# Norms of the second network taken tile by tile: squares on ACT from PSUM, transposes by tile in two banks, the next weight split between the tiles

## The reference

```python
def block(x, ...):                       # 256 x 1024
    sh1, sc1, ga1, sh2, sc2, ga2 = modulation(c)
    h = rmsnorm(x, g_mix_pre) * (1 + sc1) + sh1
    y = hybrid_mixer(h)                  # h @ w_in (1956 wide), 3 kinds of attention, @ w_out
    x = x + ga1 * rmsnorm(y, g_mix_post)
    h = rmsnorm(x, g_ffn_pre) * (1 + sc2) + sh2
    y = swiglu(h)                        # h @ w_gate_up (2 x 2816), silu(g) * u, @ w_down
    x = x + ga2 * rmsnorm(y, g_ffn_post)
```

## Time and profile before

| | us |
|---|---|
| median of 3 runs | 2006.28 (2004.70 to 2008.29) |
| profiled execution, its own time | 2009.39 |
| its span in the trace | 2007.6 |
| PE busy | 1788.9 (89%) |
| DVE busy | 1121.1 (56%) |
| ACT busy | 688.0 (34%) |
| POOL busy | 96.2 (5%) |
| mean granted clock of PE | 0.917 |

### The profile page before, as it was taken

One profiled execution on the slowest core, in us unless ns is written; L12 is line 12 of the kernel. 1 busy time (PEld: TensorE's weight loads), 2 busy tenths in 40 slices (PEclk: granted clock), 3 DMA queues, 4 the chain that ended last, 5 costly groups with the idle time before them and its releaser, 6 DMA issues.

```text
span 2007.6 us, 25506 instructions
## 1 busy us (share of the span) xinstructions
PE 1788.9 (89%) x10612; PEld 1454.1 (72%) x10612; DVE 1121.1 (56%) x1727; ACT 688.0 (34%) x811; POOL 96.2 (5%) x91
## 2 busy tenths in 40 slices
PE   5998888789999999988879996997899979879997
PEld 2775646677877777775558995775799756759996
DVE  3475454564445445555477675555766565566654
ACT  2323333132222122423334443454333333534331
POOL 1010001110000000010010000000100010010000
PEclk8999877899999999897889998898899989879999
DMA  8324455124333344334754545450555554325642
GB/s 325 124 86 168 169 197 202 42 75 149 133 126 126 129 159 144 105 136 147 257 192 171 203 175 206 151 190 10 161 187 164 180 199 152 126 63 182 196 159 93
DMA packets 172371, 309.20 MB, mean 154 GB/s; under 512 B 3264, under 2 KB 54720, under 8 KB 171616
## 3 DMA queue, kind: packets, MB, share of 16 engines
q1 hardware_dynamic: 168592, 293.98, 42.1%
q10 hardware_dynamic: 3376, 12.02, 1.8%
q0 software_dynamic: 288, 1.57, 0.2%
HBM read 305.46 MB, written 2.10 MB: 153 GB/s over the span
## 4 chain that ended last, share of the span: by engine, by line
PE 69%; DVE 16%; ACT 5%; issue 5%; DMA 3%; POOL 1%; DVEq 0%; ACTq 0%; SPq 0%; POOLq 0%
PE bank L535 53%; PE twin L535 14%; DVE ring_r L1159 4%; DVE arena L1159 3%; PE bank L544 3%; ACT arena L1884 2%; ACT arena_r L1884 2%; DMA ring<-in_w_in 2%; DMA ring<-in_w_mod 2%; POOL rs L2235 1%; DVE params L1159 1%; DVE arena_r L1159 1%; DVE X L1636 1%; DVE params L1622 0%; DVE arena L1249 0%
## 5 line engine op out<-in xcount | busy, mean ns | idle before, releaser
L535 PE MATMUL bank<-arena_r 128*128 128x512 f32 (+3 forms) x2144 | 710.2, 377 | 14.5 <-DVE arena_r L1754 6.7
L1159 DVE TENSOR_TENSOR ring_r<-ring,arena_r 128x4096 fp32r<-128x4096 f32 (+4 forms) x94 | 393.7, 4188 | 233.3 <-ACT arena_r L1884 232.7
L535 PEld LDWEIGHTS bank<-arena_r 128*128 128x128 f32 x2144 | 412.2, 192 | 95.8 <-issue 7.9
L1884 ACT ACTIVATE arena_r<-ring 128x4096 fp32r<-128x4096 f32 (+4 forms) x94 | 323.0, 3436 | 432.9 <-PE bank L535 160.5
L535 PE MATMUL twin<-actT_r,arena_r 128*128 128x256 f32 x1408 | 254.5, 284 | 1.2 <-DVE actT_r L1159 1.2
L535 PE MATMUL bank<-arena_r,actT_r 128*128 128x512 f32 (+4 forms) x640 | 227.1, 386 | 25.7 <-DVE ring_r L1159 14.2
L535 PE MATMUL bank<-ring_r,arena_r 128*128 128x512 f32 x624 | 246.0, 394 | 0.0
L1884 ACT ACTIVATE arena<-bank 128x512 f32<-128x512 f32 (+6 forms) x170 | 85.7, 504 | 426.2 <-PE bank L535 329.8
L535 PEld LDWEIGHTS twin<-actT_r,arena_r 128*128 128x128 f32 x1408 | 219.8, 192 | 2.0 <-DVE actT_r L1159 2.0
L535 PE MATMUL twin<-actT_r,ring_r 128*128 128x256 f32 x704 | 199.2, 283 | 0.0
L535 PE MATMUL bank<-ring_r,actT_r 128*128 128x512 f32 (+4 forms) x512 | 191.7, 374 | 0.0
(11 more groups left out here) (183 smaller groups left out, 1753.0 us busy)
## 6 DMA issues: line engine op xcount, KB each, us to landing
ring<-in_w_mod SPq DMA_DIRECT2D x24, 2048.0 KB, 8.0
ring<-in_w_ada SPq DMA_DIRECT2D x24, 2048.0 KB, 8.2
ring<-in_w_gate_up SPq DMA_DIRECT2D x44, 1024.0 KB, 7.7
ring<-in_w_down SPq DMA_DIRECT2D x20, 2048.0 KB, 7.8
ring<-in_w_up SPq DMA_DIRECT2D x16, 2048.0 KB, 7.8
ring<-in_w_in SPq DMA_DIRECT2D x12, 2048.0 KB, 8.7
ring<-in_w_out SPq DMA_DIRECT2D x8, 2048.0 KB, 11.7
ring<-in_w_down SPq DMA_DIRECT2D x8, 1792.0 KB, 7.5
```

The lines of the kernel that those rows point to most:

```text
L535: ins = nc.tensor.matmul(out_, lhsT, rhs, start=start, stop=stop)
L1159: return v.tensor_tensor(o, x, y, op)
L1884: return nc.scalar.activation(o, x, func, **kw)
```

## The change

Six things change, all for the second network:

1. `residual2`: DVE no longer copies the banks nor squares them. ACT squares the sums straight from PSUM (`squares2`), with the accumulated sum in `ss`, and DVE multiplies straight from the bank by `GA`, once `gsq_ready` says that ACT's square is there.
2. `residual2` now does in half 1, for tile 0 and then tile 1: half of the next weight's split (`split_part`), the scaling, the addition to `X`, and `norm_tile`. For tile 1 `turned2(0)` stands between the addition and the norm.
3. PE transposes a tile at a time (`normed2` on PE): feature tiles 0 to 3 of tile t in one v bank, 4 to 7 in one a bank, in a burst of 8 for t = 0 and one for t = 1.
4. `turned2(t)` on DVE and `normed2` on ACT empty these: four 128x128 scale-and-shift each, one rounding copy of 128x512 each, and two subtractions of 128x512, both on DVE. POOL has no part in it any more.
5. The next product waits for `act_ready`: for `in2` 0 its first tile of tokens needs only tile 0; for `up2` 0, which takes both tiles at once, the first feature tile needs the third and the fifth the fourth of the four signals.
6. In `loads()` the first `mod2` chunk of a layer stands behind `in2` 0 instead of ahead of it.

```diff
-        out += [("par2a", l, 0)] + take(1) + ins[:3] + [("par2b", l, 0)] + take(1) + ins[3:] + take(2)
+        out += [("par2a", l, 0)] + ins[:1] + take(1) + ins[1:3] + [("par2b", l, 0)] + take(1) + ins[3:] + take(2)
```

PE, the transposes (here and below B's call stands for the three):

```diff
+            def normed2(n):
+
+                for t in range(TS):
+                    pe.wait_ge(xn_ready, nth(xn_ready))
+                    for g, r in enumerate("va"):
+                        b, filled = take(r)
+                        for i in range(4):
+                            ft = 4 * g + i
+                            tr(b[:, i * P:(i + 1) * P], normal(n)[:, t, ft * P:(ft + 1) * P], filled if i == 3 else None)
...
-                normed([0, 1], 2 * (L + l) + 1)
+                mark["y", l, 1] = k["v"]
+                normed2(2 * (L + l) + 1)
```

DVE:

```diff
+            def turned2(t):
+
+                c = slice(t * P, (t + 1) * P)
+                b = filled()
+                for ft in range(4):
+                    step(v.tensor_scalar(act2_lo[:, ft, c], b[:, ft * P:(ft + 1) * P], modT[:, 1, ft, 0:1],
+                                         modT[:, 0, ft, 0:1], ALU.mult, ALU.add), v_emptied if ft == 3 else v_step)
+                step(v.tensor_copy(actT_r[:, 0:4, c], act2_lo[:, 0:4, c]))
+                rest(act2_lo[:, 0:4, c], act2_lo_r[:, 0:4, c], actT_r[:, 0:4, c], act_ready)
+                dve.wait_ge(high_ready, nth(high_ready))
+                rest(act2_lo[:, 4:8, c], act2_lo_r[:, 4:8, c], actT_r[:, 4:8, c], act_ready)
...
             def last_norm(t):
+                if t == 1:
+                    turned2(0)
                 dve.wait_ge(sq_ready, nth(sq_ready))
...
                 for half in range(2):
                     c = slice(half * MODC, (half + 1) * MODC)
                     for key in keys[half]:
-                        split(after(key))
+                        if key != keys[1][-1]:
+                            split(after(key))
...
                     for t in range(TS):
-                        b = filled()
-                        y = y2[:, t, c]
-                        step(v.tensor_copy(y, b[:, :]), v_emptied)
-                        squares(junk2, y, t)
...
+                        if half and late:
+                            split_part(late, t, False)
+                        scaled(t, half)
+                        if half:
+                            added(t)
+                            if n and t == 1:
+                                turned2(0)
+                            if n:
+                                norm_tile(t, n)
+                if n:
+                    turned2(1)
```

ACT, where `squares2` is called once for each half, behind the last high part of that half:

```diff
+            def squares2(l, stage, half):
+
+                n = mark["y", l, 2 * stage + half] - 2
+                for t in range(TS):
+                    act.wait_ge(v_filled, n + t + 1)
+                    step(f(junk2, VB[(n + t) % 2][:, :], ACT.Square, accum_out=ss[:, 2 * half + t:2 * half + t + 1]),
+                         gsq_ready)
+
+            def normed2(n):
+
+                for t in range(TS):
+                    squared([t], n)
+                    if t == 0:
+                        act.wait_ge(modT_ready, nth(modT_ready))
+                    c = slice(t * P, (t + 1) * P)
+                    b = filled()
+                    for i in range(4):
+                        step(f(act2_lo[:, 4 + i, c], b[:, i * P:(i + 1) * P], ACT.Identity, scale=modT[:, 1, 4 + i, 0:1],
+                               bias=modT[:, 0, 4 + i, 0:1]), a_emptied if i == 3 else a_step)
+                    step(f(actT_r[:, 4:8, c], act2_lo[:, 4:8, c], ACT.Copy), high_ready)
```

More of the change, by code:

```diff
@@ L570, in three, with linear @@
                 mm(out_, lhs[1], rhs[0], False, last, inc)
-            def linear(out_, lhs, rhs, inc, order=range(KT)):
+            def linear(out_, lhs, rhs, inc, order=range(KT), turned={}):
                 for i in order:
+                    if i in turned:
+                        pe.wait_ge(act_ready, nth(act_ready, turned[i]))
                     if k["turned"]:
@@ L1225, in split, with split_part @@
                             ALU.subtract), w_ready)
-            def split_part(key, part):
-                if part:
+            def split_part(key, part, parted=True):
+                if part or not parted:
                     dve.wait_ge(whi_ready, SPLITS.index(key) + 1)
@@ L1607, in squares, with residual2, scaled, added @@
                                             op1=ALU.add, accum_out=ss[:, at:at + 1]))
-            def residual2(keys, behind):
+            def residual2(keys, late, n):
                 dve.wait_ge(ga_in, nth(ga_in, 32))
+                def scaled(t, half):
+                    c = slice(half * MODC, (half + 1) * MODC)
+                    b = filled()
+                    mean = ms[:, t:t + 1]
+                    dve.wait_ge(gsq_ready, nth(gsq_ready))
+                    if half == 0:
+                        step(v.tensor_scalar(mean, ss[:, t:t + 1], 1.0 / D, EPS, ALU.mult, ALU.add))
+                    else:
+                        v.scalar_tensor_tensor(out=mean, in0=ss[:, 2 + t:3 + t], scalar=1.0 / D, in1=mean,
+                                               op0=ALU.mult, op1=ALU.add).then_inc(ms_ready, 1)
+                        handed.append(("power", t, 1))
+                    step(tt(y2[:, t, c], b[:, :], GA[:, 0, c], ALU.mult), v_emptied)
+                def added(t):
+                    dve.wait_ge(rstd_ready, nth(rstd_ready))
+                    step(v.scalar_tensor_tensor(out=X[:, t, :], in0=y2[:, t, :], scalar=rs[:, t:t + 1],
+                                                in1=X[:, t, :], op0=ALU.mult, op1=ALU.add), x_ready)
                 for half in range(2):
@@ L1619, in residual2 @@
                     for t in range(TS):
[L1620 to L1639 removed]
+                        if half and late:
[9 more added lines that the diff above has]
+                    turned2(1)
             def layer2(l):
[L1642 removed]
+                if l == 0:
+                    turned2(1)
                 split(after(("in2", l, 0)))
@@ L2205, in layer2 @@
                     split(after(("down2", l, c)))
+                    if c % 3 == 2:
+                        squares2(l, 1, c // 3)
             act.dma_start(cons[:, :], a["cons"]).then_inc(cons_in, 16)
```

43 lines of the change are left out of this document (16 added, 27 removed).

## The result

The changed kernel is slower: 2022.1 us (median of 7 runs, 2014.18 to 2026.03) against 2006.2 us for the kernel before (7 runs, 1999.5 to 2009.31). The ratio is 1.0075, 95% interval 1.0058 to 1.0093. The forecast was 2015.4 with a range up to 2021.5: the median lies 0.6 above that end, and the ratio, on the 2006.28 that the forecast was made from, gives 2021.3, just inside it.

A forecast was written before the change was run, and what follows sets the result against it. PE was taken as the bound (busy 89%, chain of waits 69% on PE, 16% on DVE). A -0.8, B and D +10.0, C +1.9, E -2.0 sum to +9.1, on the median 2006.28 giving 2015.4 us; range 2006.5 to 2021.5.

The forecast's parts named there:

- B: PE's idle time ahead of the norm's transposes between `out2` and `up2` in layer 0; predicted +5.0 us.
- F: The time at which the last product of `out2` ends, from which the prediction counts its chain of steps.
- A: PE's idle time ahead of the transposes before `in2` 0 in layer 0; predicted -6.3 + 5.5 = -0.8 us.
- D: The same place as B in layer 1, taken as its twin; predicted +5.0 us.
- C: The same place as A in layer 1; predicted -2.0 - 0.3 + 4.2 = +1.9 us.
- E: The kernel's end, where DVE's copy and square of tile 1 go; predicted 1.7 earlier and 0.3 for half 0: -2.0 us.
- Rival 3: PE stays at the low clock 7 us behind each burst pair; B and D lose 2.5 more each, C 2: 2022; chance 0.13.
- (i): At B and D, ScalarE's order holds tile 0's norm back until behind F; mending it gives about -6 us in all.
- (ii): At B and D, the half split of 2.3 us stands on the path; splitting whole gives -4.7 us in all.
- (iii): At B and D, `turned2(0)`'s 3.6 us stand in the way of tile 1's norm; reordering gains 7 us in all.
- (iv): At A and C, `in2` 2 is late because its load takes `in2` 0's slot; the old order removes 5.9 us waits: 2019 to 2023.

## Why the prediction was right, and where not

**The direction and the mechanism were right.** At B each step of the chain came where the prediction put it:

| step | predicted | measured |
|---|---|---|
| square of `X` tile 0 there | F + 2.3 | F + 2.0 |
| norm of tile 0 | F + 4.0 | F + 3.6 |
| half split | F + 6.2 | F + 6.0 |
| addition of tile 1 | F + 8.7 | F + 8.2 |
| `turned2(0)` | F + 12.2 | F + 11.9 |
| norm of tile 1 | F + 13.8 | F + 13.5 |
| four transposes of tile 1, seen by VectorE | F + 15.1 | F + 14.8 |
| first product | F + 17.9 | F + 17.8 |

That the last step fits within 0.1 is partly luck, since small errors cancel: ScalarE's two squares were 0.3 shorter than I had put them, the four 128x128 took 1.75, not 1.45, and the rounding copy 0.43, not 0.6.

**The terms**, in the first pair of profiles: A -0.6 (predicted -0.8), B +5.6 (+5.0), D +6.2 (+5.0), C +1.5 (+1.9), E -0.3 for half 0 and -1.9 for the last addition (-2.0 together). `in2` 2's product came at S + 19.9 in both layers, predicted S + 19.2, with S the issue of its load.

That A and C fit so well is luck. At A the first product with `in2` 0 came 7.3 sooner, not 6.3, and what followed cost 6.8, not 5.5. At C S came 2.8 sooner, not 2.0, and the rest cost 4.6, not 4.2. I had overlooked that the load of `in2` 2 waits not for the last product with `in2` 0 but for the first one with `in2` 1, 1.3 and 1.6 us later. And C is +1.5 only beside the first profile of before, where the clock fell from 1679 to 1683; beside the second, where it did not, it is +3.4.

With 1.6 for `down2` behind D (below) the terms add up to 12.2, and the pair differs by 8.6. The other 3.6 lie between the places, where no instruction differs: 1.1 ahead of B, 1.5 ahead of C, where before the clock fell from 1587 to 1591, and 1.0 ahead of D. At E the addition ends 3.1 us behind the last product (which ended at 2004.85) where it was 5.0 (1998.17), as this row shows beside the earlier trace rows:

```profile
2006.66 1.28 DVE L1661 SCALAR_TENSOR_TENSOR X<-params,rs,X 128x1024 f32<-128x1024 f32 x1
```

**The term that was mis-sized is the clock.** I had put 0.9 at each of B and D. The 1056 products took 128.7 us at B and 129.3 at D, and 126.9 where they ran at the high level throughout (at D with TensorE kept busy): 1.8 and 2.4. `down2`'s second half behind D took 1.6 more as well: in both profiles of the changed kernel the clock fell again there, in neither of before. This is that place in the first one:

```profile
1974.00:1976.00 2.00, 2.00 (x6) 1.51 (x6) 0.00 (x0) 1.92 (x1) 0.00 (x0) 0.52 0.75 254
```

But this fall is no sure part of the price. In both profiles of before the same fall of 3.4 us stands in `down2` of layer 0, 174 us behind F at B, and in neither of the changed kernel; and the changed kernel with the whole split, or with the loads of before, has it in neither layer. The runs show that such a fall comes at the same place in both profiles of a kernel, not what sets it off.

Rival 3 had the direction, that the clock costs more than 0.9, and the total, 2022, but not by its own working: it wanted 2.5 more at each of B and D, which were 0.9 and 1.5, and 2 more at C.

**What stays open.** The medians lie 15 to 16 us apart, the stretches behind A give 8.6 to 9.9. So the sum, 9.1, fits what lies behind A and not the whole difference. Some 3 us more lie ahead of A, where no instruction differs: the pass ended at 1235.8 to 1245.4 (mean 1242.0) in the eight profiles of kernels whose work by tile begins at A and at 1235.6 to 1240.1 (mean 1238.9) in the five others. The difference is TensorE's clock between 300 and 400 us and between 1000 and 1100 us, where TensorE is busy at the low level for 24 to 36 us, and for 8 to 16. Both ends occur in both groups. Whether the change shifts their odds, or eight against five profiles were luck, is not settled; nor are the last 3 us.

**The theories inside the sum:** (i) shown, (ii) shown, (iii) refuted, (iv) shown. What the prediction lacked was the look ahead of F. There VectorE's order, not the amount of its work, decides: the part that looked like the gain was worth nothing at B and D until the gates went ahead of the split and the split was cut to fit the waits. Which of these two edits gave how much of the 3.2 us was not run apart.

## What to carry to other kernels

When work is cut into tiles, write down each in-order engine's list around the point where the last input arrives, and look for an instruction whose input is ready standing behind one whose input is not; here one such line cost 2.4 and 3.0 us at two places. Cutting a step in two has its price too: here half the columns cost four fifths of the time, POOL no longer shared the work, and TensorE got two short bursts in place of one. Filler work (a weight's split) belongs in pieces where the engine waits anyway.

## What the runs showed of the hardware

- A short stretch between fixed events repeats (F to the last `up2` product: 140.94 to 140.96 us over four readings), while the time of the kernel before varied by 15 us over the 54 runs beside the experiments: the shortest, 1996.0, had a mean granted clock of 0.926, the longest, 2011.2, one of 0.918. The clock goes with the time but does not fix it: a run of 2008.4 had 0.922.
- VectorE's 128x128 from a bank costs 0.44 us where 128x256 costs 0.54: half the columns save a fifth.
- Two bursts of 8 transposes with 8.7 us idle between them left the changed kernel's streams at the low level for 4.0 us (B) and 5.4 us (D) in both profiles; in its variants without filler products it was 3.2 to 6.0. One burst of 16 left the stream at the low level for 0 to 2.6 us in the eight streams of the kernels that have it. There it cost nothing that can be read: in the two profiles of before D's stream ran low for 0.0 and 2.4 us, and its end was the same within 0.02.
- A load of 2 MB took 8.1 and 8.0 us from issue to landing in the changed kernel, with nothing else on the queue.
